# Attention steps with turns in upper bank halves, and the last two phases in one block, in a decoder layer kernel

## The reference

```python
h = rms_norm(x, pre_norm_w) * (1.0 + scale) + shift
proj = h @ w_in
q, k, v, g, gate_lr, z, xbc, dt_raw = split(proj)
o = gla_chunked(q * DK ** -0.5, k, v, log_sigmoid(gate_lr @ gla_gate_w2 + gla_gate_b) / 16)
o = rms_norm(o, gla_norm_w) * silu(g)
xbc = silu(causal_depthwise_conv(xbc, conv_w, conv_b))
y = ssd_chunked(xs, softplus(dt_raw + dt_bias), -exp(a_log), Bm, Cm) + d_skip * xs
y = grouped_rms_norm(y * silu(z), ssd_norm_w)
mixed = concatenate([o, y]) @ w_out
x = x + gate * rms_norm(mixed, post_norm_w)
```

## Time and profile before

| | us |
|---|---|
| median of 3 runs | 1736.94 |
| lowest and highest | 1735.49, 1740.21 |
| the profiled execution | 1735.65 |
| its span, first to last instruction | 1733.9 |
| PE busy | 1629.3 (94% of the span) |
| DVE busy | 1056.9 (61%) |
| ACT busy | 842.6 (49%) |
| POOL busy | 388.8 (22%) |

### The profile page before, as it was taken

One profiled execution on the slowest core, in us unless ns is written; L12 is line 12 of the kernel. 1 busy time (PEld: TensorE's weight loads), 2 busy tenths in 40 slices (PEclk: granted clock), 3 DMA queues, 4 the chain that ended last, 5 costly groups with the idle time before them and its releaser, 6 DMA issues. The chain is left out here.

```text
span 1733.9 us, 27410 instructions
## 1 busy us (share of the span) xinstructions
PE 1629.3 (94%) x10022; PEld 1400.9 (81%) x10022; DVE 1056.9 (61%) x1752; ACT 842.6 (49%) x1496; POOL 388.8 (22%) x449
## 2 busy tenths in 40 slices
PE   5799899998989999997999999999999979999996
PEld 5687778887878888886888887788888868888885
DVE  4443444455554454445767777886777753785995
ACT  5555555545544554453455445655544544234332
POOL 5000100010242222200223232222323220451421
PEclk9999999999999999998999999999999999999998
DMA  9423162253433543344113224422222325665885
GB/s 279 157 87 109 44 183 67 74 164 117 152 128 122 170 146 122 122 131 149 50 68 110 73 73 126 129 80 71 107 73 73 102 101 182 228 243 170 287 284 181
DMA packets 131358, 231.14 MB, mean 133 GB/s; under 512 B 9907, under 2 KB 81859, under 8 KB 126134
## 3 DMA queue, kind: packets, MB, share of 16 engines
q1 hardware_dynamic: 121830, 189.71, 33.7%
q10 hardware_dynamic: 8592, 39.85, 6.3%
q0 software_dynamic: 832, 0.22, 0.2%
HBM read 177.05 MB, written 52.70 MB: 133 GB/s over the span
## 5 line engine op out<-in xcount | busy, mean ns | idle before, releaser
L1100 PE MATMUL ps<-hl,w 128*128 128x512 f32 x1488 | 377.4, 403 | 0.1
L1100 PEld LDWEIGHTS ps<-hl,w 128*128 128x128 f32 x1488 | 277.6, 191 | 57.8 <-issue 1.4
L1780 PE MATMUL ps<-hl,w 128*128 128x256 f32 x2304 | 294.7, 288 | 5.8 <-PEq L271 5.0
L1780 PEld LDWEIGHTS ps<-hl,w 128*128 128x128 f32 x2304 | 282.4, 193 | 14.1 <-issue 13.1
L1106 PE MATMUL ps<-w,hl 128*128 128x256 f32 x1536 | 201.5, 288 | 2.0 <-DVE w L799 2.0
L1106 PEld LDWEIGHTS ps<-w,hl 128*128 128x128 f32 x1536 | 191.4, 192 | 4.8 <-DVE w L799 2.4
L1658 DVE SCALAR_TENSOR_TENSOR c_acc<-c_before,conv_col,c_acc 128x256 f32<-128x256 f32 x288 | 161.6, 563 | 46.0 <-ACT c_acc L1525 39.0
L1784 PE MATMUL ps<-hl 128*128 128x512 f32 x768 | 178.6, 391 | 0.0
L2154 PE MATMUL ps<-w,hl 128*128 128x512 f32 x720 | 166.5, 393 | 5.1 <-PEq L1358 5.1
L1784 PEld LDWEIGHTS ps<-hl 128*128 128x128 f32 x768 | 143.0, 188 | 29.3 <-DVE hl L1627 0.2
L2154 PEld LDWEIGHTS ps<-w,hl 128*128 128x128 f32 x720 | 136.9, 190 | 34.0 <-issue 5.3
(11 more groups left out here) (247 smaller groups left out, 2622.3 us busy)
## 6 DMA issues: line engine op xcount, KB each, us to landing
x_sb<-h SPq DMA_DIRECT2D x52, 512.0 KB, 4.0
w_raw<-in_w_in SPq DMA_DIRECT2D x42, 512.0 KB, 4.2
c_ac<-step_sums ACTq DMA_DIRECT2D x16, 1024.0 KB, 4.6
d_a_raw<-mixed_in SPq DMA_DIRECT2D x29, 512.0 KB, 3.9
c_h_raw<-h SPq DMA_DIRECT2D x56, 256.0 KB, 2.8
d_a_raw<-mixed_in SPq DMA_DIRECT2D x11, 1024.0 KB, 5.2
w_sums<-late ACTq DMA_DIRECT2D x8, 1280.0 KB
w_raw<-w_sums SPq DMA_DIRECT2D x40, 256.0 KB, 3.3
```

Of the source, the lines that this page charges most:

```text
L1100: mm = pe.matmul(ps[:, PROJ + u % 2, :], w[:, u, k, a, :], hl[:, par, k, b, :], start=(k == 0 and i == 0), stop=(k == KT - 1 and i == 2))
L1780: mm = pe.matmul(ps[:, PROJ + u % 2, 0:B2], w[:, u, k, a, :], hl[:, par, k, b, :], start=(k == 0 and i == 0), stop=(k == KT - 1 and i == 2))
```

## The change

1. The turned k goes to the upper half of bank O (`k_turned`, columns 256 to 383 of bank 4), always; the turned outputs go to the upper half of bank KV (`o_turned`, bank 5). So bank O is read by ACT alone and bank KV by DVE alone.
2. The waits follow: `scores` waits for `on_ready` of the tile before instead of `y_ready`; the matmul into KV in `outputs` waits for `y_ready` as well; `turn` waits for `state_ready` of its own tile instead of `kt_ready`.
3. x is turned into two banks, even k into 7, odd k into 2, and `turn_x(k)` waits for the reader of k - 2 instead of k - 1.
4. `ssd` and `project_out` return their five lists instead of opening a block each, and one block runs both. Instead of the meeting of all engines, single waits: SP waits for the DMAs of y as before and for `h_ready`; PE waits for `h_ready` and `xd_ready` before j = 2 and for `y_stored` before j = 4; ACT and POOL wait for `y_stored`. `first_products` now increments `unit_done` when one of its two products is complete, which ACT waits for before its first two copies.

No instruction of PE, DVE, ACT, POOL or SP moves past another; only waits change and the branches of one block boundary go.

```diff
-    PROJ, TURNS, STEP, O, KV, LEFT, CODES = 0, 2, 3, 4, 5, 6, 6
+    PROJ, X_TURNS, STEP, O, KV, LEFT, CODES = 0, (7, 2), 3, 4, 5, 6, 6
...
-        def k_turns(r):
-            return TURNS if r + 1 < NB or r + 1 in (SIZES_AT, GATE_AT + 1) else LEFT
+        k_turned, o_turned = ps[:, O, DV:DV + DK], ps[:, KV, DV:2 * DV]
...
                     wait(pe, kt_ready, m)
-                    if k_turns(r) == TURNS:
-                        wait(pe, y_ready, m)
+                    wait(pe, on_ready, m)
                     cols = slice(t * P, (t + 1) * P)
-                    pe.transpose(ps[:, k_turns(r), 0:DK], k_end[:, cols], ident[:, :]).then_inc(kt_done, 1)
+                    pe.transpose(k_turned, k_end[:, cols], ident[:, :]).then_inc(kt_done, 1)
...
                     wait(pe, state_ready, m)
+                    wait(pe, y_ready, m)
                     pe.matmul(ps[:, KV, 0:DV], k_tok[:, :], v[:, t, :], start=True, stop=True).then_inc(kv_done, 1)
...
                     pe.wait_ge(on_ready, m + 1)
-                    pe.wait_ge(kt_ready, m + 1)
+                    pe.wait_ge(state_ready, m + 1)
                     wait(pe, y_ready, m)
                     for f in range(2):
-                        mm = pe.transpose(ps[:, TURNS, f * P:(f + 1) * P], o_n[:, f * P:(f + 1) * P], ident[:, :])
+                        mm = pe.transpose(o_turned[:, f * P:(f + 1) * P], o_n[:, f * P:(f + 1) * P], ident[:, :])
...
-                                else:
-                                    full_ready(pe, m, i - 5)
-                                turn_x(m, i - 4, LEFT + 1)
+                                if i >= 6:
+                                    full_ready(pe, m, i - 6)
+                                turn_x(m, i - 4, X_TURNS[i % 2])
...
+        with nc.Block() as block:
+            @block.sync
+            def _(sp):
+                recurrence[0](sp)
+                projection[0](sp)
...
+            @block.tensor
+            def _(pe):
+                recurrence[4](pe)
+                projection[4](pe)
...
+                if j == IN_TAIL:
+                    pe.wait_ge(h_ready, quarters_h)
+                    pe.wait_ge(xd_ready, tiles)
+                if j == HALVES_IN_TAIL:
+                    pe.wait_ge(y_stored, stores)
                     wait(pe, a_ready, j + 1 - HALVES_IN_TAIL)
...
                 act.wait_ge(consts_ready, 2)
+            act.wait_ge(y_stored, stores)
+            act.wait_ge(h_ready, quarters_h)
                 for j in range(IN_TAIL):
+                act.wait_ge(unit_done, units + j + 1)
                     copy(j)
```

More of the change, by code:

```diff
@@ L1880, with project_out @@
 TWICE = 1
-def project_out(nc, x, w_out, out, ps, gate_d, y_d, w_sum_d, w_raw, spare, halves, w_even, w_odd, D, KT, NB2, TB2):
+def project_out(nc, sems, y_stored, unit_done, h_ready, xd_ready, units, quarters_h, stores, tiles, x, w_out, out, ps, gate_d, y_d, w_sum_d, w_raw, spare, halves, w_even, w_odd, D, KT, NB2, TB2):
     HB, HN = 4, 512
@@ new lines, in gpsimd, with combine, a_sum, rstd_of @@
+        def gpsimd(pool):
+            pool.wait_ge(y_stored, stores)
+            pool.wait_ge(h_ready, quarters_h)
+            pool.memset(neg_half[:, :], -0.5).then_inc(consts_ready, 1)
+            pool.memset(ms[:, :], 0.0).then_inc(consts_ready, 1)
+            pool.wait_ge(consts_ready, 2)
+            def combine(first, second, signs):
+                if signs == (1, 1):
+                    return pool.tensor_tensor(first, first, second, ALU.add)
+                if signs == (1, -1):
+                    return pool.tensor_tensor(first, first, second, ALU.subtract)
+                return pool.tensor_tensor(first, second, first, ALU.subtract)
+            def a_sum(j):
+                terms = a_terms(j)
+                if len(terms) == 2:
+                    pool.wait_ge(a_loaded[j % RAWS], a_count(j))
+                    combine(a_term(j, 0), a_term(j, 1), (terms[0][2], terms[1][2])).then_inc(a_summed, 1)
+            def rstd_of(m):
+                pool.wait_ge(ms_ready, m + 1)
+                wait(pool, rstd_ready, m)
+                pool.tensor_scalar(mse[:, :], ms[:, :], EPS, None, ALU.add).then_inc(mse_ready, 1)
+                pool.wait_ge(mse_ready, m + 1)
+                wait(pool, scaled_ready, m)
+                pool.tensor_tensor(rstd[:, :], mse[:, :], neg_half[:, :], ALU.pow).then_inc(rstd_ready, 1)
+            for j in range(IN_TAIL, N):
+                if j + 3 < N:
+                    a_sum(j + 3)
+                for m in range(len(rows)):
+                    if square_at[m] == j:
+                        rstd_of(m)
@@ new lines, in vector, with a_low, w_low, add @@
+        def vector(dve):
+            def a_low(j):
+                dve.wait_ge(a_hi, j + 1 - HALVES_IN_TAIL)
+                half = halves[:, j % 4]
+                dve.tensor_tensor(half[:, :, LO, :], a_term(j, 0).rearrange("p (f n) -> p f n", n=P),
+                                  half[:, :, HI, :].bitcast(F32), ALU.subtract).then_inc(a_ready, 1)
+            def w_low(v):
+                i, f = v // KT + 1, v % KT
+                dve.wait_ge(w_hi, v + 1)
+                dve.tensor_tensor(weight(i)[:, f, LO, :], w_part(v), weight(i)[:, f, HI, :].bitcast(F32),
+                                  ALU.subtract).then_inc(w_ready, 1)
+            def add(j):
+                i, p = j // NB2, j % NB2
+                terms = [(r, c, how) for (r, c), how in PRODUCTS[i][2] if how != 0]
+                if not terms:
+                    return
+                wait(dve, prod_done, j + 1 - IN_TAIL)
+                wait(dve, added, adds(j - NB2))
+                dve.wait_ge(copied, copies(j if any(how == 0 for _, how in PRODUCTS[i][2]) else j - NB2))
+                bank = ps[:, j % 8, :]
+                for r, c, how in terms:
+                    old = mixed[:, p, 0, 1, :] if i == TWICE else mixed[:, p, r, c, :]
+                    last = dve.tensor_tensor(mixed[:, p, r, c, :], old, bank, ALU.add if how > 0 else ALU.subtract)
+                last.then_inc(added, 1)
+            def finish(m):
+                r, p = rows[m]
+                row = mixed[:, p, r].rearrange("p c n -> p (c n)")
+                dve.wait_ge(rstd_ready, m + 1)
+                if m == 0:
+                    dve.wait_ge(gate_loaded, 16)
+                dve.scalar_tensor_tensor(out=row, in0=row, scalar=rstd[:, :], in1=gate_row[:, :], op0=ALU.mult,
+                                         op1=ALU.mult).then_inc(scaled_ready, 1)
+                dve.wait_ge(scaled_ready, m + 1)
+                dve.wait_ge(x_loaded[m % XS], (m // XS + 1) * 16)
+                dve.tensor_tensor(row, row, x_sb[:, m % XS, :], ALU.add).then_inc(sum_ready, 1)
+            for j in range(IN_TAIL, N + 1):
+                if j + 2 < N:
+                    a_low(j + 2)
+                for m in range(len(rows)):
+                    if square_at[m] + 1 == j:
+                        finish(m)
+                for v in W_AT.get(j, ()):
+                    w_low(v)
+                if j < N:
+                    add(j)
@@ new lines, in tensor @@
+        def tensor(pe):
+            for j in range(IN_TAIL, N):
+                i = j // NB2
+                if j == IN_TAIL:
[3 more added lines that the diff above has]
+                    pe.wait_ge(y_stored, stores)
+                wait(pe, a_ready, j + 1 - HALVES_IN_TAIL)
+                wait(pe, copied, copies(j - 8))
+                wait(pe, added, adds(j - 8))
+                for k in range(KT):
+                    if i > 0 and j % NB2 == 0:
+                        pe.wait_ge(w_ready, (i - 1) * KT + k + 1)
+                    for q, (a, b) in enumerate(PASSES):
+                        mm = pe.matmul(ps[:, j % 8, :], halves[:, j % 4, k, a, :], weight(i)[:, k, b, :],
+                                       start=(k == 0 and q == 0), stop=(k == KT - 1 and q == 2))
+                mm.then_inc(prod_done, 1)
```

1200 lines of the change are left out of this document (563 added, 637 removed).

## The result

The changed kernel takes 1713.4 us (median of 4 runs, 1712.7 to 1714.0) against 1737.8 for the kernel before on the same chip: a ratio of 0.9868, 95% interval 0.9854 to 0.9883, 24.4 us less by the medians and 22.9 by the ratio (20 to 25). The forecast was 1715, which is 21.8 us less. The profiled execution took 1712.74, its span 1711.0 against 1733.9.

The account below looks back on a forecast made before the run. PE, busy 94% of the span, sets the pace. Gains of 7.5 (x), 6.3 (k and outputs) and 8.0 us (boundary), together 21.8, take the profiled 1735.65 to 1713.9, or 1715 as a median; range 1711 to 1718, chance 0.55.

Parts of the forecast that it names:

- The front: The turns of x and those of k and outputs, ahead of the recurrence: 7.5 and 6.3 us gained.
- the boundary: Between recurrence and projection: 5.35 us of idle time and 2.75 of lower clock gained, 0.1 lost, 8.0 in sum.
- Turns of x: Steps 0 to 2: four stalls for `x_full` shorten, ending with L765 instead, and the clock stays up: 7.5 us gained.
- The 3.0 us of clock: Part of the 7.5 us for x, in steps 0 and 1: PE no longer runs at its lower clock.
- Turns of k and outputs: Six stalls for y, 9.5 us, go; the mask or `dec` is late next in four: 6.3 us gained.
- (d): Rival: the lower clock after 394.3 and some of `dec` go too, 4 us more gained: 1710; chance 0.06.
- the feed of j = 4: Projection: operands loaded after the stores of y land arrive about when PE wants them; 0.1 us lost for the feed.
- (a): Rival: PE still slows down at 77, 142 and 1424, so 5.8 us of clock are missing: 1721; chance 0.2.
- (b): Rival: a chain that PE does not pace takes the front's gain back, all but some 3 us: 1726; chance 0.08.
- (c): Rival: the projection starves, loads late for j = 4 to 8, 4 us lost: 1719; chance 0.06.
- (e): Rival: PE fetches code anew at each turn of the recurrence's hardware loops; slower, up to 1785; chance 0.03.
- (f): Rival: the new waits at boundary and front hold PE as long as the old stalls: 1737; chance 0.02.

Follow-up runs that it names:

- e3: The changed kernel, but x is turned into bank 7 alone and each turn waits for the reader of k - 1: 1720.3 us.
- e1: The kernel before, with only recurrence and projection joined in one block: 1730.8 us.
- e6: The kernel before, with 16 filler matmuls on PE behind the last turns of the recurrence: 1733.8 us.
- e8: The kernel before, with the product `codes` made one slot later: 1736.6 us.
- e2: The changed banks and waits, with recurrence and projection in two blocks as in the kernel before: 1720.7 us.
- e4: The changed kernel, but the turn of k also waits for y of the tile before, in all 60 tiles: 1760.7 us.
- e5: The changed kernel, but PE waits for the stores of y before the products j = 2 instead of j = 4: 1722.9 us.
- e9: The changed kernel, with four of GpSimd's five sums of `w_out` moved from the end of step n = 8 into the next step: 1707.3 us.
- e11: The changed kernel, unaltered, measured again: 1714.3 us.
- e12: The changed kernel with the sums moved as in e9 and `codes` one slot later in steps 1 and 2 only: 1701.2 us.
- e7: The changed kernel, with the product `codes` made one slot later: 1707.2 us.
- e10: The changed kernel with the edits of both e7 and e9: 1701.2 us.

## Why the prediction was right, point by point

The mechanism of each term held, and the sizes mostly. That the whole is within 1.1 us of the forecast in the ledger (22.9 against 21.8) is in part luck. The front gave 3.4 us that the sum did not hold (1.8 of stalls, 1.6 of clock behind them) and the boundary 1.0 less than forecast; the rest, 1.3 us of loss, is scatter of the two executions (+1.25 before 68 us, -1.0 at 492, +1.0 in the recurrence).

**Turns of x (7.5).** Found 7.4 in the ledger, step by step as worked out, and 6.9 by e3. That the stall does not vanish but ends with L765 was the step that carried it: waits of 1.79, 2.23 and 2.21 us were found where 1.7 and 2.3 stood in the text. The 3.0 us of clock in it came too, and not by chance. Behind the stall of 2.9 us in step 0 the 12 matmuls took 3.6 to 4.5 us in all five traces that have it (before, e1, e3, e6, e8), and 2.9 us behind the stall of 1.8, in all seven traces that have that one (the changed kernel, e2, e4, e5, e9, e11, e12). In step 1 the 24 took 3.8 to 4.5 us behind 3.4 us of idle time, in five of five, and 3.0 behind 2.2, in six of six. Step 2 is the exception (last section).

**Turns of k and outputs (6.3).** The mechanism held: no wait for y is left, L1174 and L1182 never wait for y or the state, `dec` stands at 10.7 us as forecast (10 to 12), and the two waits of the mask are there. The size was low, 8.1 against 6.3. The whole stalls at slots 3 and 6 gave 1.3 and 0.6 to 0.7 (taken: 1.16 and 0.47), with 0.3 more just behind the first; the two at slot 9 gave 1.9 to 2.0 (1.84 each), those at slot 0 0.6 each, with 0.2 more behind one (0.51 each), and a wait of 0.93 us before L1137 at 384.55 shrank to 0.62 (not counted at all). The remainder at slot 9, 0.36 both times in place of 0.43, is the nearest of them. What the sum left out at each whole stall is 0.15 us beyond its idle time: a turn that waits for nothing starts before the modelled end of the matmuls ahead (at 242.47, they end at 239.51 + 3.12 = 242.63), and a turn that waits loses this overlap as well (2.42 us for the stall of 2.27).

**The clock behind those stalls.** The matmuls after 394.3 gave 1.6 us that the sum did not hold; they stood in rival (d), which with this came true in part. The gain is no chance of this execution. In each of the five traces that have the stalls of 2.3 us at 394 and at 431, the matmuls behind exactly one of the two are slow, 4.6 us for 3.0 or 3.1 (before and e8 at 394; e1, e4 and e6 at 431). In the nine others, where 1.7 us remain at the one place and none at the other, never. I had counted the clock as gained where a stall lost 1.1 us, and not here, where one lost 0.6 and the other all: no reason in the rows for that distinction. The 1.0 us at 492 stood behind a stall that the change left as it was, and is scatter.

**The boundary (8.0).** Idle time 5.39 (5.35) and clock 2.5 (2.75) nearly as forecast; the feed of j = 4 costs a wait of 0.66 us, 0.9 in the ledger, not 0.1. The step that was too tight is the time at which SP goes on: I put it 2.2 us behind the issue of the last store. SP's queue in the changed kernel:

```profile
1405.68 0.54 SPq L1416 DMA_DIRECT2D mixed_in<-c_y_diff  x1
1408.47 0.34 SPq L1993 DMA_DIRECT2D d_a_raw<-mixed_in  x1
```

From the one to the other it is 2.79 us, not less than the 2.5 that landing and meeting took together before: the part that I gave the meeting is not to be seen, and the landing varies by tenths. In e1 the wait was 0.38, in e7 and e9 0.2, in e10 and e12 there is none. PE stands nowhere else in the projection.

**Rivals.** (a), that the clock stays down at 77, 142 and 1424, falls at all three: at the boundary by e6 and by the row of 1403, at the other two by the traces counted above. In step 2, where the forecast had put no clock term, the lower clock comes and goes. (b) falls by e2. (c) had a true core of 0.66 us. (e), that the hardware loops fetch code anew, falls: the recurrence stays within 1 us of its length. (f) falls.

## What to carry to other kernels

When a wait is taken away, look for the next instruction of the same engine and for when its own operand is ready: that end, not the length of the removed wait, gave the idle time of every term here within some tenths. Look also at how fast the matmuls run behind the stall: of the 22.9 us of the ledger about 7 were clock. An edit that is worth nothing (e8) may be worth 6 us once the wait ahead of it is gone, and the other way round, so measure a chain of edits in its order. Ahead of a boundary between two stages, ask which of its waits the first work behind it needs; often it is none.

## What was not expected of the hardware

- **The same stall, two clocks.** The changed kernel and its second measurement are one program. Both stand 2.21 us for `h_low` in step 2. The two windows 194 to 197 (busy time of PE, PEld, DVE, ACT, POOL, granted clock, DMA share), the changed kernel first, e11 second:

```profile
194.00:197.00 3.00, 3.00 (x28) 3.00 (x27) 1.07 (x3) 1.37 (x3) 0.00 (x0) 1.00 0.45 175
```

```profile
194.00:197.00 3.00, 3.00 (x12) 2.82 (x13) 1.88 (x4) 1.30 (x2) 0.00 (x0) 0.50 0.28 107
```

  One runs at 2.4 GHz (granted clock 1.00), the other at 1.2 (0.50), and it costs 1.4 us in the ledger. Of the six traces with this stall of 2.2 us three run on at full clock (the changed kernel, e2, e4) and three do not (e5, e9, e11). Behind the stall for `w_low` in step 0 the changed kernel takes 3.13 us for 24 matmuls, the stall being 1.04 us; e9 and e12 take 4.64 and 4.63 behind 1.03 and 1.06, at the lower clock. And the 3.37 us of idle time in step 2, which the kernel before and four runs have, cost no clock in two of the five traces (before, e6). At the three places of the forecast the shorter stall kept the clock up in every trace; how far that goes elsewhere is not shown. The advice on idle gaps that the prediction cites from the Trainium skill (TensorE: Matmul & The Clock Gate, "Why this matters for your kernels") holds here as a tendency and not for a given stall, by these numbers. What decides in the single case stays open.
- **VectorE beside GpSimd**: 1.74 to 1.77 us for an operation of 0.68, and GpSimd's five sums take 8.12 us, where one alone takes 1.31 in e9. The 4.1 us that VectorE lost were nearly all of PE's longest wait of 4.56.
